# Half-size-product chunks: weight sums placed behind the down updates, silu products last

## The reference, cut to what matters

```python
def swiglu(x, w_gate, w_up, w_down):
    return (jax.nn.silu(x @ w_gate) * (x @ w_up)) @ w_down

for l in range(2):
    x = x + 0.5 * swiglu(rms_norm_2(x, ffn1_norm[l]), ffn1_w_gate[l], ffn1_w_up[l], ffn1_w_down[l])
    ...
    x = x + 0.5 * swiglu(rms_norm_2(x, ffn2_norm[l]), ffn2_w_gate[l], ffn2_w_up[l], ffn2_w_down[l])
```

## Time and profile before

| what | us |
|---|---|
| median of 3 runs (lowest to highest) | 3432.93 (3432.87 to 3434.36) |
| the profiled execution | 3428.76 |
| its span, from the first to the last instruction | 3427.0 |
| TensorE busy in the span | 3336.7 (97%) |
| VectorE busy | 2187.3 (64%) |
| GpSimd busy | 2092.3 (61%) |
| ScalarE busy | 1463.6 (43%) |
| mean granted clock of TensorE | 0.994 of full |

### The profile page before, as it was taken

The page is one execution under the profiler, slowest core; times in us unless marked ns, Lnnn a source line. Parts: engine busy times, 40 slices in busy tenths (PEclk is TensorE's granted clock), DMA queues, the critical chain, the costliest instruction groups (busy, mean ns, idle before and its releaser), DMA issues.

```text
span 3427.0 us, 52738 instructions
## 1 busy us (share of the span) xinstructions
PE 3336.7 (97%) x17742; PEld 2818.0 (82%) x17742; DVE 2187.3 (64%) x3377; ACT 1463.6 (43%) x2025; POOL 2092.3 (61%) x2188
## 2 busy tenths in 40 slices
PE   9999999999999999999999999999999999999998
PEld 5888777888888887888888888888887888888888
DVE  8886785444577768614337777777778334347776
ACT  4465673222333336635633333433347545443332
POOL 6443445555577775554367776687766543558775
PEclk9999999999999999999999999999999999999999
DMA  6222543322232222332223222232223222223222
GB/s 222 86 68 68 178 154 119 104 93 97 92 109 101 86 86 93 99 123 68 69 98 119 93 94 78 92 105 98 86 86 111 93 100 67 86 99 111 86 98 92
DMA packets 94485, 343.36 MB, mean 100 GB/s; under 512 B 10609, under 2 KB 11249, under 8 KB 93954
## 3 DMA queue, kind: packets, MB, share of 16 engines
q1 hardware_dynamic: 86978, 312.11, 26.5%
q10 hardware_dynamic: 7360, 29.29, 2.6%
HBM read 335.03 MB, written 2.13 MB: 98 GB/s over the span
## 4 chain that ended last, share of the span: by engine, by line
POOL 37%; PE 31%; issue 26%; DVE 3%; ACT 2%; DVEq 1%; POOLq 0%; ACTq 0%; DMA 0%
POOL w_lo L588 35%; PE ps L634 9%; PE ps L636 8%; PE ps L635 8%; POOL t_lo L588 1%; PE ps L1217 1%; PE ps L1199 1%; PE ps L801 1%; PE ps L802 1%; PE ps L803 1%; DVE arena L2761 0%; PE ps L1208 0%; DVEq L2763 0%; ACT w_hi L1305 0%; DVE arena L2172 0%
## 5 line engine op out<-in xcount | busy, mean ns | idle before, releaser
L588 POOL TENSOR_TENSOR w_lo<-raw,w_hi 128x256 fp32r<-128x256 f32 (+1 forms) x1680 | 1460.3, 901 | 1152.4 <-ACT w_hi L1305 1053.0
L634 PE MATMUL ps<-a_hi,w_lo 128*128 128x512 f32 (+1 forms) x2720 | 1021.2, 375 | 13.0 <-POOL w_lo L588 5.1
L636 PE MATMUL ps<-a_hi,w_hi 128*128 128x512 f32 (+1 forms) x2720 | 1005.4, 370 | 0.0
L635 PE MATMUL ps<-a_lo,w_hi 128*128 128x512 f32 (+1 forms) x2720 | 1005.0, 369 | 0.0
L588 POOL TENSOR_TENSOR w_lo<-arena,w_hi 128x512 fp32r<-128x512 f32 x384 | 556.6, 1474 | 158.8 <-ACT w_hi L1785 156.0
L634 PEld LDWEIGHTS ps<-a_hi,w_lo 128*128 128x128 f32 x2720 | 512.5, 188 | 118.6 <-issue 28.5
L636 PEld LDWEIGHTS ps<-a_hi,w_hi 128*128 128x128 f32 x2720 | 512.4, 188 | 88.1
L1305 ACT ACTIVATE w_hi<-raw 128x1024 fp32r<-128x1024 f32 x374 | 392.6, 1053 | 443.2 <-PE ps L636 424.6
L635 PEld LDWEIGHTS ps<-a_lo,w_hi 128*128 128x128 f32 x2720 | 512.9, 189 | 81.4 <-issue 0.5
L634 PE MATMUL ps<-b_hi,w_lo 128*128 128x512 f32 x1088 | 425.9, 391 | 4.8 <-DVE b_lo L2190 4.0
L635 PE MATMUL ps<-b_lo,w_hi 128*128 128x512 f32 x1088 | 423.9, 390 | 0.0
(11 more groups left out here) (330 smaller groups left out, 4823.3 us busy)
## 6 DMA issues: line engine op xcount, KB each, us to landing
raw<-in_stream SPq DMA_DIRECT2D x471, 512.0 KB, 3.3
arena<-in_stream SPq DMA_DIRECT2D x96, 512.0 KB, 3.4
arena<-in_mod_w ACTq DMA_DIRECT2D x32, 512.0 KB, 4.2
arena<-in_mod_w SPq DMA_DIRECT2D x16, 512.0 KB, 11.5
arena<-arena ACTq DMA_DIRECT2D x16, 256.0 KB, 3.7
arena<-cum_rows ACTq DMA_DIRECT2D x2, 2048.0 KB, 7.9
xres<-in_x_t SPq DMA_DIRECT2D x4, 512.0 KB, 5.1
arena<-in_first SPq DMA_DIRECT2D x8, 256.0 KB, 11.8
```

The source lines that it names most:

```text
L588: last = pool.tensor_tensor(to[:, at], of[:, at], hi[:, at].bitcast(F32), ALU.subtract)
L634: pe.matmul(out, lo, x_hi, start=start, stop=False)
L635: pe.matmul(out, hi, x_lo, start=False, stop=False)
L636: return pe.matmul(out, hi, x_hi, start=False, stop=stop)
```

## The change

It moves VectorE's instructions and removes none. In a loop chunk all eight sums leave their places and one stands behind each of the eight updates, the four of gate first, then the four of up. The two hidden tiles come after all of that. In chunk 7 the six instructions of the hidden tiles stand one behind each of updates 0 to 5. Ahead of the loop the sums of chunk 0 stand partly between the last updates of the third plain chunk: gate sum 2 behind update 4, gate sum 3 behind update 5 (with a wait for the third of the four low parts of x's sums), up sum 0 behind update 6. `fast_hidden` now drains ahead of each step and calls no `hidden` (which makes the high and the low part with a drain ahead of each). The lines of `sums` move by one: L2636 is L2637.

```diff
--- before.py
+++ after.py
@@ -2518,12 +2518,13 @@
                 y = v_tile()
                 dve.scalar_tensor_tensor(xres[:, m, :], y, scale, xres[:, m, :], ALU.mult, ALU.add).then_inc(dve_evacuated, 1)
 
-            def add_tiles(scales, squares=False):
-
-                for m, scale in scales:
+            def add_tiles(scales, squares=False, beside=lambda n: None):
+
+                for n, (m, scale) in enumerate(scales):
                     if squares and m == KT - 1:
                         add_square(m - 1)
                     add_tile(m, scale)
+                    beside(n)
                     if squares and 0 < m < KT - 1:
                         add_square(m - 1)
 
@@ -2672,36 +2673,36 @@
                 dve.wait_ge(fast_done, c.fast.at(15 + m))
                 dve.scalar_tensor_tensor(xres[:, k, :], ps[:, bank, :], scale, xres[:, k, :], ALU.mult, ALU.add).then_inc(down_read, 1)
 
-            def fast_hidden(half, m):
-
-                if m == 0:
+            def fast_hidden(half, m, step):
+
+                t, n = tt[:, m, :], 2 * half + m
+                dve.drain()
+                if step == 0:
                     dve.wait_ge(gate_silu, c.gate_silu.at(2))
-                t = tt[:, m, :]
-                dve.tensor_tensor(t, sgate[:, m, :], ps[:, UP_BANKS[2 * m], :], ALU.mult).then_inc(up_read, 1)
-                hidden(half, m, t)
+                    dve.tensor_tensor(t, sgate[:, m, :], ps[:, UP_BANKS[2 * m], :], ALU.mult).then_inc(up_read, 1)
+                if step == 1:
+                    dve.tensor_copy(a_hi[:, n, :], t)
+                if step == 2:
+                    dve.tensor_tensor(a_lo[:, n, :], t, a_hi[:, n, :].bitcast(F32), ALU.subtract).then_inc(hidden_ready, 1)
 
             def fast_chunk(last):
 
                 gate_banks = fast_banks(c.part.n)
                 assert (c.dve.n + c.dve.shift) % WIDE == FAST_BANK[c.part.n]
                 combine(gate_banks, 6, 1, gate_m1, gate_u4).then_inc(gate_ready, 1)
-                if not last:
-                    sums("gate", 0, 3, 1)
                 combine(UP_BANKS, 12, 2, up_m1, up_u4)
                 combine_last(gate_banks, 13, gate_m1, gate_u4).then_inc(gate_ready, 1)
                 combine_last(UP_BANKS, 14, up_m1, up_u4)
-                if not last:
-                    sums("gate", 3, 4, 1)
                 for m in range(8):
                     fast_down(m)
-                    if last and m in (1, 4):
-                        dve.drain()
-                        fast_hidden(1, m // 4)
-                dve.drain()
+                    if last and m < 6:
+                        fast_hidden(1, m // 3, m % 3)
+                    if not last:
+                        sums("up" if m >= 4 else "gate", m % 4, m % 4 + 1, 1)
                 if not last:
                     for m in range(2):
-                        fast_hidden(0, m)
-                    sums("up", 0, 4, 1)
+                        for step in range(3):
+                            fast_hidden(0, m, step)
                 dve.drain()
                 c.fast.n += FAST_TILES
                 c.fast_raw.n += 16
@@ -2730,16 +2731,21 @@
                     if n == 2:
                         dve.wait_ge(turns_ready, 4 * c.part.n + 1)
                         sums("gate", 0, 2, 0)
-                    if n == 3:
+
+                def third_beside(n):
+                    if n == 4:
                         sums("gate", 2, 3, 0)
+                    if n == 5:
+                        dve.wait_ge(turns_ready, 4 * c.part.n + 3)
+                        sums("gate", 3, 4, 0)
+                    if n == 6:
+                        sums("up", 0, 1, 0)
 
                 ffn_up(0, second_beside)
                 dve.drain()
-                add_tiles(ffn_out)
+                add_tiles(ffn_out, beside=third_beside)
                 dve.memset(cols[:, 126:127], 0.0).then_inc(normalised, 1)
-                dve.wait_ge(turns_ready, 4 * c.part.n + 4)
-                sums("gate", 3, 4, 0)
-                sums("up", 0, 4, 0)
+                sums("up", 1, 4, 0)
                 dve.drain()
                 with loop(dve, FAST - 1, c, fast=FAST_TILES, fast_raw=16, fast_lo=FAST_UNITS, gate_silu=2):
                     fast_chunk(False)
```

## The result

The changed kernel takes **3352.66 us** (median of 4 runs, 3352.11 to 3353.28), the kernel before 3432.9 (4 runs, 3432.01 to 3434.36). The ratio is 0.9766, with a 95% interval from 0.9749 to 0.9783: 80.2 us or 2.3% less. The forecast was 3362 with a range from 3344 to 3397.

What follows compares the result with a forecast made beforehand. TensorE was taken as the bound, with only its waits to win. 72.5 + 9.2 + 6.8 + 5.6 + 3.9 - 26.6 = 71.4 us off the profiled 3428.76 gives 3357, plus 4.2 for the median: 3362 us, range 3344 to 3397.

Steps and rivals of the forecast that it cites:

- Unit 4 and the 2 us wait: Loop chunks, third up product: moving up sums frees unit 4 by 10.7 us, so TensorE's 2.04 us wait goes.
- The new wait at down 4: Loop chunks, down stage: sums between updates delay TensorE 0.95 us in each of 28 chunks, 26.6 us added.
- The rival of 1.6 us for each met sum: Down stage: each sum meeting GpSimd takes 1.6 us, the wait grows to 2.2 us, result 3395; chance 0.18.
- The hidden tiles: Loop chunks: tiles end at 9.6 us, unit 5 hidden by 0.3 us; rival of late tiles 3376, chance 0.15.
- The clock: Slow stretches in chunks after the 2.04 us waits vanish with those waits, 6.8 us off; lower bound 0.
- The ends: Work ahead of the loop and in the last chunks: terms of 5.6 and 3.9 us off.
- The term ahead of the parts: Ahead of the loop: earlier gate sums 2 and 3 remove the 0.83, 0.41 and 0.15 us waits, 5.6 us.
- the 0.41 us wait: Chunk 0 of each part: a TensorE wait expected to go because ScalarE can round unit 2 earlier.
- The term for the last chunks: Chunk 7, down stage: down 4 no longer waits for a whole hidden tile, 4 x 0.96 = 3.9 us off.
- That takes the 0.30 us wait with it: Loop chunks: gate sums leaving their place behind the first combination stop slowing GpSimd, so the 0.30 us wait goes.
- Half of the new waits absent: Range's lower end: half of the new waits absent and the rest as forecast, given as 3344.
- the closing figures: Chances stated last: faster 0.93, same 0.03, slower 0.04; the list before had slower 0.03, no change 0.04.

Runs made afterwards that it cites:

- the run with the up sums alone: Kernel before with only the four up sums moved behind updates 4 to 7 of the loop chunks; 3343.41 us against 3432.92, ratio 0.9739.
- the filler: Kernel before with 16 unused matmuls ahead of the third up product of chunks 1 to 7; 3421.05 us against 3432.92, ratio 0.9967.
- up sums and ends: Changed kernel with its gate sums back in their old place behind the first and last combinations; 3333.57 us, ratio 0.9711 to the kernel before.
- two early: Changed kernel with gate sums 0 and 1 behind the first combination, the other six sums behind updates 2 to 7; 3329.33 us, ratio 0.9700.
- the copy free as well: Gate sums 0 and 1 early, plus ScalarE's wait for hidden tiles moved from the first gate block's copy to the first silu; 3327.04 us, ratio 0.9692.
- the run with the gate sums alone: Kernel before with only the four gate sums moved behind updates 0 to 3 of the loop chunks; 3434.14 us against 3432.92, ratio 1.0003.
- the sums one update later: Changed kernel with each of the eight sums one update later; 3373.71 us against 3432.54 for the kernel before, ratio 0.9828.

## Why the prediction was right, and where it was not

**Unit 4 and the 2 us wait: right.** Counted from the chunk's first product (1177.02 us), the trace has unit 4 rounded at 5.95 (forecast 5.8), GpSimd at it at 7.52 (7.5) and the unit there at 10.69 (10.7). The run with the up sums alone shows that this part makes the whole gain: 89.5 us. The 7.5 was reached with some luck: the row it is read from gives 1193.56 - 1186.3 = 7.3, and the trace comes out at 7.52 because GpSimd's four passes there now take 6.13 us in place of 5.88.

**The new wait at down 4: right.** Counted from the moment down 0 is ready, gate sum 0 ended at 2.2 us (forecast 2.2), gate sum 1 at 3.9 (4.0), update 2 at 4.5 (4.6). The loss per chunk is 31.70 - 30.76 = 0.94 us (forecast 0.95, 26.6 us in all), of which the idle column shows 0.6. The rival of 1.6 us for each met sum fell: the medians in the changed kernel are 1.19 and 1.01, and what sets them is the end of the pass, as shown above.

**The hidden tiles: right.** They ended 9.5 us after the first product (forecast 9.6), unit 5 was not waited for, and one more sum between the last update and them did make it late. The slack was underrated: unit 5's low half was there at 13.55 us (forecast 13.9), 0.65 ahead of TensorE and not 0.3.

**The clock: mis-sized.** The step was "the nine long distances less 33.78 each, 6.8 us in all". It left out two slow stretches in last chunks, where no distance to a next chunk shows them: less their long distances, the second and the fourth part of before take 1.4 and 1.5 us more than the first and third. With them the profile of before holds 9.7 us. And the runs behind the median are slower still than the profiled one (4.2 us); the filler measures 11.9 us (7 to 16) for the clock in the median. The 2.9 us and the 4.2 us make 7.1 of the error of 9.3 us: the profiled one of before was a lucky execution, and adding its 4.2 us back to the forecast was wrong, since the changed kernel, with no such stretch, has its median at its profiled time.

**The ends: right in sum.** The term ahead of the parts was 4 x 1.4 = 5.6 us, and the stretches there gave 4.6: of the 0.41 us wait 0.16 is left. The term for the last chunks was 3.9 us, and they gave 4.9: 1.2 us each, from their first combination to their last update, between the up sums alone and up sums and ends. The sum is 9.5 either way, and the medians of these two kernels differ by 9.8.

**"That takes the 0.30 us wait with it": the failed reason.** In the forecast the gate sums had to leave their place for that wait to go. With the gate sums left there it went all the same. So moving the gate sums was not needed, and the 0.94 us per chunk which I priced so closely was a cost without a return; of that half only the sums behind updates 2 and 3 earn something, the 4.2 us above. The forecast came out right because it priced the change as made; it would have misjudged the simpler one: 31.5 us a chunk were expected of it and 30.97 came, 15 us over 28 chunks.

**Two slips in the forecast's working.** Half of the new waits absent makes 3362 - 13.3 = 3349 us, so the lower end of the range, 3344, does not follow from the reason given for it. And the closing figures have the chances of "same" and "slower" the other way round than the list in front of them. Neither touches the result.

**The last 0.1 to 0.2 us of a chunk in the versions with early gate sums** can be read from their traces, counted from a chunk's first product. TensorE comes to unit 6 at 17.0 us and to unit 7, the first of down, at 19.9. With four gate sums early GpSimd has them ready at 16.95 and 19.91 us, so TensorE restarts behind both, and a chunk takes 30.98. With two early only unit 6 is that close (unit 7 is there at 19.5), and it takes 30.88. With the copy free as well unit 6 is there at 16.6, and it takes 30.78. These restarts are too short for the idle column; that each costs 0.1 us is read from these three versions and not from a run made for it.

## What to carry to other kernels

When a late instruction holds up one unit of a chain, move that instruction first and read the profile again before moving its neighbours: waits downstream of it may go by themselves. Work put between updates must fit the slack in front of the first bank that comes round again, counted with the price it has beside the other engine, not its price alone. Here that price was what is left of the other engine's pass plus 0.55 us, so it can be worked out from the two timelines. And where TensorE stands idle, price the clock apart from the idle time, over several executions and not from one profile.

## What the runs showed of the hardware

TensorE's granted clock fell after an idle time of only 2.04 us. In the profile of before this happened at 11 of 28 such places, in the run with the gate sums alone at 4 of 28, with the places filled by matmuls at none. At 8 of the 11 the first matmul behind the wait, of 256 columns, takes 0.58 us in place of 0.39 (the lower level, 1.2 GHz); at the other three it takes 0.38 to 0.44, and the level falls 0.2 to 0.8 us behind its start. The window to the next such place has a granted clock of 0.95. It costs 0.7 to 0.8 us in the loop chunks of before, and 1.4 to 1.5 in its last chunks and in the run with the gate sums alone. Idle times of 0.1 to 0.6 us never did it in the changed kernel. Why the same idle time lowers the clock in one chunk and not in the next is open; it was not tried.

A VectorE sum of 128x512 with both operands in SBUF takes 0.69 us alone, and ends 0.55 us after GpSimd's pass when it begins inside one. The updates, with one operand in PSUM, keep their 0.68 or 0.69 us beside the same passes.

An idle time in the column is less than what it costs: 2.34 against 3.02 us a chunk before, 0.61 against 0.94 in the changed kernel, 0.85 against 1.7 with the sums one update later. The sum of products and downs against the distance between chunks is the safer measure.
